# Shorter heads and ten Strassen pairs in a retention and HGRN2 layer on one core

## The chip, the core and the metric

The kernel runs on one core of a Trainium2 chip. The time is device microseconds of that core, from one launch of the whole layer. Five engines work side by side and meet through semaphores: TensorE (PE in the profile, its weight loads PEld), VectorE (DVE), ScalarE (ACT), GpSimd (POOL) and SyncE (SP), which here issues nearly all DMAs.

## The reference

One layer of a streaming encoder, in float32, for 1024 frames of a new stream and 8 x 16 frames of running streams (1152 frames in all, 9 tiles of 128), model width 1024:

```python
h = rms_norm(x, g_pre_mix)
z = h @ w_in                                   # 1024 x 10240
q_a, k_a, v_a, g_a, q_b, f_b, i_b, g_b, m_a, m_b = split(z)
# branch a: retention, 4 heads of 256, q and k rotated (rope), chunk-recurrent state
o_a = head_rms(retention(rope(q_a), rope(k_a) / 16, v_a, s_ret))
y_a = (silu(g_a) * o_a) @ w_a
# branch b: HGRN2, 8 heads of 128, forget gate f, state S_t = diag(f_t) S_(t-1) + k_t v_t^T
o_b = head_rms(hgrn2(q_b, 1 - f, i_b, log f, s_hgrn))
y_b = (silu(g_b) * o_b) @ w_b
x = x + rms_norm((sigmoid(m_a) * y_a + sigmoid(m_b) * y_b) @ w_out, g_post_mix)
u = square(relu(rms_norm(x, g_pre_ffn) @ w_up))
x = x + rms_norm(u @ w_down, g_post_ffn)
```

The outputs are x for both sets of frames and the new states of all heads.

## The kernel before

Every product in float32 is made of three products of the `fp32r` type: each operand is split into a high part (a rounded copy, made by ScalarE: `WHI`, `XH`) and a remainder (made by VectorE: `WLO`, `XL`), and the three cross products are summed in PSUM.

The input projection `z` is made in blocks of 128 output columns. Two kinds of block exist:
- a **plain block** (`gemm`) takes three **slots**, one for each chunk of 384 frames; a slot is 8 x 3 = 24 products of 384 columns. ScalarE copies each finished slot to `ZST` (`evac`), SyncE stores the block to `scratch_z`. For the next block ScalarE makes `WHI` and VectorE `WLO` (`wlo_block`), once in three slots.
- a **Strassen pair** (`strassen`) makes two blocks at once with seven half-size products instead of eight: 7 x 2 halves x 4 x 3 = 168 products of 288 columns. `NZ` pairs run in a stage of their own ahead of the retention; the pairs are the blocks of `z` that come first in `z_item`.

The heads of both branches have small products that depend on VectorE, ScalarE and GpSimd. They are woven into the plain blocks, so that TensorE has a slot of work between two dependent steps. The order is written out by hand as a function of the slot number `s` within a head:
- a retention head has `RET_BLOCKS` = 6 blocks, 18 slots. From slot `RA` = 7 on, tile `t` is started in slot 7 + t (`ret_a`: transpose of the keys, scores), finished in the next slot (`ret_b`: output and state, for the last tile `ret_b8` with the eight streams' states), and its output is transposed another slot later (`out_t`). Ahead of that VectorE rotates the head's queries (`rotate_q`, three chunks) and half of its keys (`rotate_k0`), GpSimd the other half. Then `q_ok` and `k_ok` let `ret_a` begin.
- an HGRN head has `HG_BLOCKS` = 4 blocks, 12 slots. Tiles are started in the slots `HG_A`, that is 0, 1, 2 and 4 to 9 (`hg_a`), with `hg_b` one slot and `out_t` two slots later. GpSimd prepares the decayed keys of each chunk of three tiles (`prep_k`), VectorE the queries (`prep_q`) and the score weights (`weights`), and the chunks 0 and 1 of the next head are begun in this head.
- behind the retention lie `GAP` = 2 blocks without head work.

Of each finished tile the path to its transpose is the same in both branches: ScalarE squares and sums (`head_sq`), VectorE makes the mean (`head_ms`, tile `OMS`), GpSimd takes the power -1/2 (`head_rs`, tile `ORS`), ScalarE scales the output (`head_scale`, tile `OT`), TensorE transposes it (`out_t`), VectorE multiplies with the gate (`gated`, tile `UB`).

Each engine works its instructions off in the order written. Behind the heads, from the block `NRB` on, follow the projections `w_a`, `w_b`, `w_out` and the feed-forward part, which the change leaves alone.

## Time and profile before

| | |
|---|---|
| runs timed | 2349.69, 2350.68, 2352.55 us; median 2350.68 |
| the profiled execution | 2349.41 us, its span 2347.6 us |
| mean granted clock of TensorE | 0.998 of full |
| busy share of the span | TensorE 99%, VectorE 59%, ScalarE 35%, GpSimd 20% |
| plain blocks of `z` and their products of 384 columns | 60, of them 58 behind the first stage; L942 to L944, 1776 of each |
| Strassen products of 288 columns | L1054 to L1057, 3360, for 6 pairs of `z` and 14 of the feed-forward part |

A busy time is the time in which at least one instruction of the engine ran; the durations of TensorE's products overlap (their ends are modelled), so what a product costs is read from start to start. A wait is put down to the instruction that came last.

### The profile page before, as it was taken

What the parts mean: (1) busy time and instruction counts of PE and PEld (TensorE: products, weight loads), DVE (VectorE), ACT (ScalarE), POOL (GpSimd) and SP (SyncE); (2) the same over time, 40 slices, a digit from 0 to 9 for tenths busy, and PEclk for the clock granted to TensorE, in tenths of its full rate; (3) what the DMA queues carried; (4) which work ended last, traced back from release to release, by engine and by line L of the source; (5) the groups of instructions that cost most, each with busy time, mean ns of one, the idle gap of its engine ahead of it and who ended that gap; (6) DMA issues with size and microseconds to landing.
All of it is one profiled execution on the core that took longest, in us unless ns stands there. A gap on an engine that the chain in (4) does not pass through costs nothing. (4 is left out here: it accounts for less than half of the span.)

```text
span 2347.6 us, 37061 instructions
## 1 busy us (share of the span) xinstructions
PE 2325.4 (99%) x14240; PEld 2184.5 (93%) x14240; DVE 1378.4 (59%) x2562; ACT 818.0 (35%) x1552; POOL 477.9 (20%) x732
## 2 busy tenths in 40 slices
PE   8999999999999999999999999999999999999998
PEld 7899999999999999999999999988999999888886
DVE  7434355362636777777776434556755556777575
ACT  5223232323222333333232332333555554333233
POOL 1000022221206666566655000000000000000002
PEclk9999999999999999999999999999999999999999
DMA  5212455353724343344334634222434436533424
GB/s 196 85 57 103 145 181 173 123 200 115 234 93 158 116 130 113 114 128 133 108 115 143 203 106 140 100 100 82 150 112 152 137 123 250 191 117 125 170 72 143
DMA packets 256044, 319.23 MB, mean 136 GB/s; under 512 B 10005, under 2 KB 200217, under 8 KB 255769
## 3 DMA queue, kind: packets, MB, share of 16 engines
q1 hardware_dynamic: 255464, 315.67, 40.1%
q0 software_dynamic: 432, 1.57, 0.4%
q8 instruction: 96, 1.57, 0.3%
q14 instruction: 52, 0.42, 0.1%
...
## 5 line engine op out<-in xcount | busy, mean ns | idle before, releaser
L942 PE MATMUL bank<-XH,WHI 128*128 128x384 f32 x1776 | 609.9, 343 | 1.6 <-issue 0.9
L944 PE MATMUL bank<-XH,WLO 128*128 128x384 f32 x1776 | 594.7, 335 | 0.0
L943 PE MATMUL bank<-XL,WHI 128*128 128x384 f32 x1776 | 593.9, 334 | 0.0
L942 PEld LDWEIGHTS bank<-XH,WHI 128*128 128x128 f32 x1776 | 333.8, 188 | 5.6 <-issue 2.4
L943 PEld LDWEIGHTS bank<-XL,WHI 128*128 128x128 f32 x1776 | 333.9, 188 | 0.8
L944 PEld LDWEIGHTS bank<-XH,WLO 128*128 128x128 f32 x1776 | 333.3, 188 | 0.0
L1396 ACT ACTIVATE ZST<-bank 128x384 f32<-128x384 f32 x180 | 88.3, 492 | 377.6 <-PE bank L944 371.8
L1330 PE MATMUL bank<-WSH,USH 128*128 128x512 f32 x448 | 175.3, 391 | 1.0 <-issue 1.0
L1332 PE MATMUL bank<-WSH,USL 128*128 128x512 f32 x448 | 175.3, 391 | 0.0
L1331 PE MATMUL bank<-WSL,USH 128*128 128x512 f32 x448 | 175.1, 391 | 0.0
L1396 ACT ACTIVATE WHI<-WRAW 128x1024 fp32r<-128x1024 f32 (+1 forms) x161 | 135.2, 842 | 114.0 <-PE bank L1057 70.3
L2604 POOL TENSOR_TENSOR ORS<-OMS,mhalf 128x1 f32<-128x1 f32 x108 | 69.8, 646 | 440.7 <-DVE OMS L2100 406.1
L2604 POOL TENSOR_TENSOR yrs<-yms,mhalf 128x1 f32<-128x1 f32 x9 | 9.4, 1215 | 708.0 <-DVE yms L2398 708.0
L1057 PE MATMUL bank<-XH,WLO 128*128 128x288 f32 x480 | 141.6, 295 | 0.0
L1057 PE MATMUL bank<-SXH,WXL 128*128 128x288 f32 x480 | 141.5, 295 | 0.0
L1056 PE MATMUL bank<-SXL,WXH 128*128 128x288 f32 x480 | 141.3, 294 | 0.0
L1056 PE MATMUL bank<-XL,WHI 128*128 128x288 f32 x480 | 141.3, 294 | 0.0
L1054 PE MATMUL bank<-SXH,WXH 128*128 128x288 f32 x480 | 141.3, 294 | 0.0
L1054 PE MATMUL bank<-XH,WHI 128*128 128x288 f32 x480 | 141.3, 294 | 0.0
L2055 DVE TENSOR_TENSOR U<-U,bank 128x288 f32<-128x288 f32 x120 | 54.3, 453 | 124.5 <-PE bank L1057 124.5
L1396 ACT ACTIVATE USH<-UOP 128x2048 fp32r<-128x2048 f32 x28 | 53.7, 1916 | 210.5 <-PE bank L1332 210.5
L1921 DVE TENSOR_TENSOR WLO<-WRAW,WHI 128x1024 fp32r<-128x1024 f32 x80 | 102.6, 1283 | 37.0 <-ACT WHI L1396 28.7
...
## 6 DMA issues: line engine op xcount, KB each, us to landing
...
```

Of the source, the lines that this page charges most:

```text
L942: pe.matmul(psum[c][:, 0:CH], WHI[p][:, k, :], XH[:, k, s], start=(k == 0), stop=False)
L943: pe.matmul(psum[c][:, 0:CH], WHI[p][:, k, :], XL[:, k, s], start=False, stop=False)
L944: last = pe.matmul(psum[c][:, 0:CH], WLO[p][:, k, :], XH[:, k, s], start=False, stop=(k == KT - 1))
L1054: pe.matmul(bank, wh[:, k, :], xh[:, k0 + k, ts], start=(fresh and k == 0), stop=False, skip_group_check=True)
L1056: pe.matmul(bank, wh[:, k, :], xl[:, k0 + k, ts], start=False, stop=False, skip_group_check=True)
L1057: last = pe.matmul(bank, wl[:, k, :], xh[:, k0 + k, ts], start=False, stop=(k == 3), skip_group_check=True)
L1330: pe.matmul(out, uh(k), wh[:, k, :], start=(fresh and k == 0), stop=False, skip_group_check=True)
L1331: pe.matmul(out, uh(k), wl[:, k, :], start=False, stop=False, skip_group_check=True)
L1332: last = pe.matmul(out, ul(k), wh[:, k, :], start=False, stop=(k == 3), skip_group_check=True)
L1396: return act.activation(dst, src, ACT.Copy)
L1921: dve.tensor_tensor(lo, src, plain(hi), ALU.subtract).then_inc(w_lo, 1)
L2604: return pool.tensor_tensor(dst, src, e, ALU.pow)
```

## The change

`NZ` goes from 6 to 10: four more Strassen pairs, eight plain blocks of `z` fewer. To have room for that, the heads get shorter: the retention has 21 blocks (6, 5, 5, 5 for its heads; `RA` becomes `RET_A`, 7 for head 0 and 4 for the others), the HGRN part 29 blocks with the two free ones ahead of it. HGRN heads no longer begin at a block's edge: seven have 10 slots, the last has 11, and `hg_slots` runs through them. Tile `t` is started in slot `t`, without a pause. The last tile's `out_t` falls into slot 0 of the next head.

What surrounds the heads moves with them. In the retention the stream states get a buffer of their own (`S8A` lay in `ZK`, the raw keys) and `KZ8` moves into `RTMP`, so that the next head's raw keys can be loaded from the fourth block of this head on. GpSimd rotates chunk 0 of the next head's keys ahead of the last tile's `head_rs` and chunks 1 and 2 behind it; VectorE rotates chunk 0 of the next head's queries in the last slot. In the HGRN part GpSimd takes the last tile's root of the old head within `prep_k` of chunk 1, and tile 0's root behind that `prep_k`. The loops over heads and pairs of heads that were rolled on the engines (`Fori`) are now written out.

```diff
@@ -38,14 +38,16 @@
 PAST = 512
 EPS = 1e-6
 
-RET_BLOCKS = 6
-RET_SLOTS = RET_BLOCKS * NC
-HG_BLOCKS = 4
-HG_SLOTS = HG_BLOCKS * NC
-RA = 7
-HG_A = (0, 1, 2, 4, 5, 6, 7, 8, 9)
-R_GATE = (7, 8, 13)
-H_GATE = (0, 2, 6)
+RET_LEN = (6, 5, 5, 5)
+RET_AT = (0, 6, 11, 16)
+RET_BLOCKS = sum(RET_LEN)
+HG_BLOCKS = 29
+HG_START = 6
+HG_LEN = (10, 10, 10, 10, 10, 10, 10, 11)
+HG_AT = [None] * HG_START + [(h, s) for h, n in enumerate(HG_LEN) for s in range(n)]
+RET_A = tuple(NC * n - 11 for n in RET_LEN)
+R_GATE = (0, 1, 6)
+H_GATE = (1, 2, 6)
 BW = P + TS
...
@@ -57,8 +59,7 @@
 NGD = 4
 NPL = 2
 NQ = FF // 256
-GAP = 2
-NZ = 7 - GAP // 2
+NZ = (72 - 2 - RET_BLOCKS - HG_BLOCKS) // 2
 NP = NZ + NQ - NPL
 VT = 2 * NT
...
@@ -180,8 +181,8 @@
         ZETA, G128, G16 = (HC[:, 4 * P + i:4 * P + i + 1] for i in range(3))
         SR = sb("SR", [P, 2, RD], F32, pr)
         S8B = sb("S8B", [P, 4, 2, RD], F32, pr)
-        S8A = ZK[:, :, :].rearrange("p a t -> p (a t)")[:, 0:4 * 2 * RD].rearrange("p (b d e) -> p b d e", b=4, d=2)
-        KZ8 = [sb(f"KZ8{i}", [P, RD], F32, pr) for i in range(2)]
+        S8A = sb("S8A", [P, 4, 2, RD], F32, pr)
+        KZ8 = [RTMP[:, :, :].rearrange("p a n -> p (a n)")[:, b * RD:(b + 1) * RD] for b in range(2)]
         pr.close()
...
@@ -328,8 +329,21 @@
 
         zs, us, x1s = scr["z"], scr["u"], scr["x1"]
         uqs, u8s, vs = scr["uq"], scr["u8"], scr["v"]
-        NRB = 2 + RET_BLOCKS * RH + GAP + HG_BLOCKS * HH
-        NHB = NRB - HG_BLOCKS * HH
+        NHB = 2 + RET_BLOCKS
+        NRB = NHB + HG_BLOCKS
+
+        def hg_slots():
+
+            for q, at in enumerate(HG_AT):
+                yield NHB + q // NC, q % NC, *(at or (None, None))
+
+        def hg_out(h, s):
+
+            if h is None:
+                return None
+            if s == 0:
+                return (h - 1, NT - 1) if h and HG_LEN[h - 1] == NT + 1 else None
+            return (h, s - 2) if 2 <= s < NT + 2 else None
         NB1 = NRB + 2 * KT
         W_OUT = NB1
         W_FFN = W_OUT + KT
...
@@ -652,26 +666,30 @@
                 sp.dma_start(HC[:, 0:2 * P], a["c_ret"][h, :, 0:2 * P]).then_inc(R.in_[0], 16)
                 sp.dma_start(ZQ[:, :, :], ret_z(h, 0)).then_inc(R.in_[0], 16)
 
+            def load_rk(h):
+
+                sp.dma_start(ZK[:, :, :], ret_z(h, 1)).then_inc(R.in_[1], 16)
+
             for i in range(2):
                 sp.wait_ge(z_st[i], 16)
             load_rq(0)
             for h in range(RH):
-                for j in range(RET_BLOCKS):
-                    n = 2 + RET_BLOCKS * h + j
...
@@ -703,11 +719,15 @@
                         for d in range(2):
                             sp.dma_start(S8B[:, :, d, :], a["state_ret"][0, 4:8, h, d * P:(d + 1) * P, :]
                                          .rearrange("b p e -> p b e")).then_inc(R.s8_in[1], 16)
+                    if j == late + 3 and h < RH - 1:
+                        sp.wait_ge(R.k_ok, h + 1)
+                        sp.wait_ge(R.q_ok, h + 1)
+                        z_stored(6 * h + 9 - 2 * NZ)
+                        load_rk(h + 1)
                     for c in range(2):
-                        if j == (4, 5)[c]:
+                        if j == late + (3, 4)[c]:
                             ret_store(h, c)
                 if h < RH - 1:
-                    z_stored(RET_BLOCKS * h + 7 - 2 * NZ)
                     sp.wait_ge(R.o_full, 9 * h + 8)
                     load_rq(h + 1)
                 else:
...
@@ -1149,10 +1174,12 @@
                     last = pe.transpose(PRB[:, e * P:(e + 1) * P], OT[:, e * P:(e + 1) * P], ident[:, :])
                 last.then_inc(K.ot, 1)
 
-            with pe.Fori(0, RH) as h:
-                for s in range(RET_SLOTS):
+            for h in range(RH):
+                RA = RET_A[h]
+                for s in range(NC * RET_LEN[h]):
                     j, c = divmod(s, NC)
-                    gemm(2 + RET_BLOCKS * h + j, None, j % 2, c)
+                    n = 2 + RET_AT[h] + j
+                    gemm(n, None, n % 2, c)
...
-                    if s in HG_A:
-                        hg_a(h, HG_A.index(s))
-                    if s - 2 in HG_A:
-                        out_t(H, h, HG_A.index(s - 2), 1)
-                    if s - 1 in HG_A:
-                        hg_b(h, HG_A.index(s - 1))
+            for n, c, h, s in hg_slots():
+                gemm(n, None, n % 2, c)
+                if (h, s) == (0, 0):
+                    pe.wait_ge(R.kv, 8 * RH + 1)
+                    pe.wait_ge(R.kz8, 2 * RH + 1)
+                    pe.wait_ge(R.att, 9 * RH + 1)
+                    pe.wait_ge(R.o_ev, 9 * RH + 1)
+                    pe.wait_ge(R.st_ev, 16 * RH + 1)
+                    pe.wait_ge(R.um, 9 * RH + 1)
+                if h is None:
+                    continue
+                if s < NT:
+                    hg_a(h, s)
+                if hg_out(h, s):
+                    out_t(H, *hg_out(h, s), 1)
+                if 1 <= s < NT + 1:
+                    hg_b(h, s - 1)
...
@@ -2139,16 +2155,18 @@
 
             dve.wait_ge(c_in, 48)
             dve.wait_ge(qxb0, 1)
-            with dve.Fori(0, RH) as h:
-                for s in range(RET_SLOTS):
+            for h in range(RH):
+                RA = RET_A[h]
+                for s in range(NC * RET_LEN[h]):
                     j, c = divmod(s, NC)
-                    n = 2 + RET_BLOCKS * h + j
+                    n = 2 + RET_AT[h] + j
                     if c == 0:
-                        wlo_block(n + 1, (j + 1) % 2)
+                        wlo_block(n + 1, (n + 1) % 2)
                     if s < 3:
-                        if s == 0:
-                            dve.wait_ge(R.in_[0], 32 * h + 32)
-                        rotate_q(h, s)
+                        if s == 0 and h == 0:
+                            dve.wait_ge(R.in_[0], 32)
+                        if s or h == 0:
+                            rotate_q(h, s)
                     if s == 3:
                         dve.wait_ge(R.in_[1], 16 * h + 16)
                         for c in range(NC):
@@ -2161,6 +2179,9 @@
                             dve.wait_ge(R.sc, 9 * h + t + 1)
                             dve.wait_ge(R.st_full, 16 * h + (t if t >= 2 else 1))
                             dve.tensor_tensor(ATT[t % 2][:, :], PSC[:, 0:P], DM[:, t // NTP, :], ALU.mult).then_inc(R.att, 1)
+                    if s == NC * RET_LEN[h] - 1 and h < RH - 1:
+                        dve.wait_ge(R.in_[0], 32 * h + 64)
+                        rotate_q(h + 1, 0)
                     if RA + 2 <= s < RA + 2 + NT:
                         gated(R, h, s - RA - 2, 2)
                     for t in range(NT):
...
@@ -2622,24 +2631,35 @@
             ch(pool.memset(QXB[:, :, :], 0.0))
             ch.reset()
             pool.sem_inc(qxb0, 1)
-            with pool.Fori(0, RH) as h:
-                pool.wait_ge(R.in_[1], 16 * h + 16)
-                pool.wait_ge(R.att, 9 * h + 1)
-                for c in range(NC):
-                    s = slice(c * CH, (c + 1) * CH)
-                    cs, sn = CS[:, 0, s], CS[:, 1, s]
-                    pool.tensor_tensor(PTMP[:, 0, :], ZK[:, 0, s], sn, ALU.mult)
-                    ch(pool.tensor_tensor(PTMP[:, 1, :], ZK[:, 1, s], cs, ALU.mult))
-                    last = pool.tensor_tensor(KR[:, 1, s], PTMP[:, 0, :], PTMP[:, 1, :], ALU.add)
-                    if c < NC - 1:
-                        ch(last)
-                last.then_inc(R.k_ok, 1)
+            def rotate_k1(c):
+
+                s = slice(c * CH, (c + 1) * CH)
+                cs, sn = CS[:, 0, s], CS[:, 1, s]
+                pool.tensor_tensor(PTMP[:, 0, :], ZK[:, 0, s], sn, ALU.mult)
+                ch(pool.tensor_tensor(PTMP[:, 1, :], ZK[:, 1, s], cs, ALU.mult))
+                last = pool.tensor_tensor(KR[:, 1, s], PTMP[:, 0, :], PTMP[:, 1, :], ALU.add)
+                if c < NC - 1:
+                    ch(last)
+                else:
+                    last.then_inc(R.k_ok, 1)
+
+            pool.wait_ge(R.in_[1], 16)
+            for c in range(NC):
+                rotate_k1(c)
+            for h in range(RH):
                 for c in range(2):
                     gate(R, h, c, 2, ZG[c][:, :, :])
                 for t in range(NT):
+                    if t == NT - 1 and h < RH - 1:
+                        pool.wait_ge(R.in_[1], 16 * h + 32)
+                        pool.wait_ge(R.att, 9 * h + 10)
+                        rotate_k1(0)
                     head_rs(R, h, t)
                     if t == 4:
                         gate(R, h, 2, 2, ZG[0][:, :, :])
+                if h < RH - 1:
+                    for c in range(1, NC):
+                        rotate_k1(c)
                 ch.reset()
 
             ret_mixed(pool)
...
@@ -2687,39 +2707,33 @@
                 ch(pool.tensor_tensor(KRH[:, s], KK[:, s], RR[:, s], ALU.mult))
...
-                        pool.wait_ge(H.att, 9 * h + 10)
-                        head_rs(H, h, 8)
-                    ch.reset()
+            def rs(h, t):
+                return lambda: head_rs(H, h, t)
+
+            def hgate(h, c):
+                gate(H, h, c, 1, HZ[3][:, c * CH:(c + 1) * CH].unsqueeze(1))
 
             prep_k(0, 0, 0)
             ch.reset()
-            with pool.Fori(0, HH // 2 - 1) as i:
-                hg_pair(i, False)
-            hg_pair(HH // 2 - 1, True)
+            for h in range(HH):
+                first = {0: rs(h - 1, NT - 1)} if h else {}
+                prep_k(h, 1, (h + 1) % 2, {**first, 5: lambda: hgate(h, 0)})
+                head_rs(H, h, 0)
+                hgate(h, 1)
+                head_rs(H, h, 1)
+                head_rs(H, h, 2)
+                pool.wait_ge(H.att, 9 * h + 4)
+                prep_k(h, 2, h % 2, {4: rs(h, 3)})
+                head_rs(H, h, 4)
+                hgate(h, 2)
+                if h < HH - 1:
+                    pool.wait_ge(H.att, 9 * h + 7)
+                    prep_k(h + 1, 0, (h + 1) % 2, {0: rs(h, 5), 3: rs(h, 6), 6: rs(h, 7)})
```

VectorE, the seam between two retention heads, before: the end of the loop over heads and, behind the branch, its start (`OMS` is the last tile's mean, `UB` its gated product, `RTMP`, `QR` the rotation of queries).

```order
L2183 SCALAR_TENSOR_TENSOR S8B<-S8B,HC,bank 128x512
L2100 TENSOR_SCALAR OMS<-OSS 128x1
L2110 TENSOR_TENSOR UB<-bank,SG 128x2x128
...
L1921 TENSOR_TENSOR WLO<-WRAW,WHI 128x1024
L2150 ISA
L2117 TENSOR_TENSOR RTMP<-ZQ,CS 128x384
L2118 TENSOR_TENSOR RTMP<-ZQ,CS 128x384
```

The same place now, from head 0 to head 1.

```order
L2204 SCALAR_TENSOR_TENSOR S8B<-S8B,HC,bank 128x512 x2
L2116 TENSOR_SCALAR OMS<-OSS 128x1
L2133 TENSOR_TENSOR RTMP<-ZQ,CS 128x384
...
L2142 TENSOR_TENSOR ZQ<-QR,HC 128x384 x2
L2126 TENSOR_TENSOR UB<-bank,SG 128x2x128
L85 ISA
L1937 TENSOR_TENSOR WLO<-WRAW,WHI 128x1024
L2133 TENSOR_TENSOR RTMP<-ZQ,CS 128x384
```

One of the three rotations of queries moved ahead of the gated product; the other two and all rotations of keys still stand behind the weight remainder `WLO`.

GpSimd at that place, now (`PTMP`, `KR` the rotation of keys, three rows a chunk; `ORS` the roots). Before, all nine rows of the rotation stood together at the head's start, ahead of its gates `SG`, and behind the last root stood nothing.

```order
L2613 TENSOR_TENSOR ORS<-OMS,mhalf 128x1 x3
L2638 TENSOR_TENSOR PTMP<-ZK,CS 128x384
L2639 TENSOR_TENSOR PTMP<-ZK,CS 128x384
L2640 TENSOR_TENSOR KR<-PTMP 128x384
L2613 TENSOR_TENSOR ORS<-OMS,mhalf 128x1
L2638 TENSOR_TENSOR PTMP<-ZK,CS 128x384
```

Three rows moved ahead of the last tile's root, six stand right behind it.

GpSimd in the HGRN part, before: the end of `prep_k` of chunk 1 (`RR` the running products, `KRH` its last result).

```order
L2673 TENSOR_TENSOR KE<-KK,RR 128x3x64
L2682 TENSOR_TENSOR RR<-RR,FT 128x3x64
L2618 ISA
L2604 TENSOR_TENSOR ORS<-OMS,mhalf 128x1
L2687 TENSOR_TENSOR KRH<-KK,RR 128x384
L2614 TENSOR_TENSOR SG<-SG,HZ 128x384
```

The same `prep_k` now, its start and its end, from head 0 to head 1.

```order
L2678 TENSOR_TENSOR FT<-HZ 128x192
L2679 MEMSET RR 128x384
L2702 TENSOR_TENSOR RR<-RR,HZ 128x192
L2613 TENSOR_TENSOR ORS<-OMS,mhalf 128x1
L2687 TENSOR_TENSOR KE<-KK,RR 128x384
...
L2693 TENSOR_TENSOR KE<-KK,RR 128x3x64
L2702 TENSOR_TENSOR RR<-RR,FT 128x3x64
L2707 TENSOR_TENSOR KRH<-KK,RR 128x384
L2613 TENSOR_TENSOR ORS<-OMS,mhalf 128x1
```

The root of tile 0 stood ahead of `KRH` and now stands behind it; the root near the start is that of the old head's last tile.

## Rows read from the trace of the kernel before

The rows are whole lines of the profile. A timeline row is: start and duration in us, engine, line of the kernel, operation, output and inputs by name, shapes, how many, and in brackets the engine's idle time ahead of it and what ended it.

**Rows 1.** The page of the kernel before: its span and the busy time of TensorE

```profile
span 2347.6 us, 37061 instructions
PE 2325.4 (99%) x14240; PEld 2184.5 (93%) x14240; DVE 1378.4 (59%) x2562; ACT 818.0 (35%) x1552; POOL 477.9 (20%) x732
```

**Rows 2.** TensorE's waits over the whole span: total, times, longest, us

```profile
PE bank L1149 <- ACT OT L1602: 1.2, 1, 1.2
PE bank L942 <- issue: 0.9, 1, 0.9
PE bank L942 <- DVE WLO L1921: 0.8, 1, 0.8
```

**Rows 3.** TensorE in order of time (start, duration, us): plain products, then Strassen products

```profile
36.21 0.33 PE L963 MATMUL bank<-XL,WHI 128*128 128x384 f32 x1
...
46.09 0.33 PE L963 MATMUL bank<-XL,WHI 128*128 128x384 f32 x1
...
148.11 0.29 PE L1056 MATMUL bank<-XL,WHI 128*128 128x288 f32 x1
...
151.69 0.29 PE L1056 MATMUL bank<-XL,WHI 128*128 128x288 f32 x1
```

**Rows 4.** VectorE in order of time, from retention head 0 to head 1

```profile
387.18 0.14 DVE L2100 TENSOR_SCALAR OMS<-OSS 128x1 f32<-128x1 f32 x1
389.56 0.42 DVE L2110 TENSOR_TENSOR UB<-bank,SG 128x256 f32<-128x256 f32 x1 [2.23 <-PE bank L1149]
392.26 1.23 DVE L1921 TENSOR_TENSOR WLO<-WRAW,WHI 128x1024 fp32r<-128x1024 f32 x1 [2.28 <-ACT WHI L1396]
393.41 0.55 DVE L2117 TENSOR_TENSOR RTMP<-ZQ,CS 128x384 f32<-128x384 f32 x1
...
398.83 0.56 DVE L2119 TENSOR_TENSOR QR<-RTMP 128x384 f32<-128x384 f32 x1
...
403.20 1.25 DVE L2119 TENSOR_TENSOR QR<-RTMP 128x384 f32<-128x384 f32 x1
...
418.96 0.56 DVE L2138 TENSOR_TENSOR KR<-RTMP 128x384 f32<-128x384 f32 x1
```

**Rows 5.** TensorE at the same seam: first gemm, first transpose of keys

```profile
389.27 0.42 PE L942 MATMUL bank<-XH,WHI 128*128 128x384 f32 x1
...
422.67 0.38 PE L1078 MATMUL bank<-ident,KR 128*128 128x128 f32 x2
```

**Rows 6.** GpSimd at the same seam: first and last of nine products for the keys

```profile
402.96 1.08 POOL L2631 TENSOR_TENSOR PTMP<-ZK,CS 128x384 f32<-128x384 f32 x1 [15.01 <-DMA ZK<-scratch_z]
...
412.84 1.89 POOL L2633 TENSOR_TENSOR KR<-PTMP 128x384 f32<-128x384 f32 x1
```

**Rows 7.** TensorE, from one HGRN head to the next

```profile
941.31 0.44 PE L942 MATMUL bank<-XH,WHI 128*128 128x384 f32 x1
...
963.38 0.27 PE L1149 MATMUL bank<-ident,OT 128*128 128x128 f32 x1
```

**Rows 8.** GpSimd, key preparation of chunk 1 at the same seam

```profile
943.75 0.74 POOL L2604 TENSOR_TENSOR ORS<-OMS,mhalf 128x1 f32<-128x1 f32 x1 [4.72 <-remote]
944.59 0.51 POOL L2658 TENSOR_TENSOR FT<-HZ 128x192 f32<-128x192 f32 x1
...
948.54 0.60 POOL L2675 TENSOR_TENSOR KE<-KK,RR 128x192 f32<-128x192 f32 x1
...
950.18 1.45 POOL L2675 TENSOR_TENSOR KE<-KK,RR 128x192 f32<-128x192 f32 x1
...
959.85 0.59 POOL L2604 TENSOR_TENSOR ORS<-OMS,mhalf 128x1 f32<-128x1 f32 x1 [2.47 <-DVE OMS L2100]
960.42 1.16 POOL L2687 TENSOR_TENSOR KRH<-KK,RR 128x384 f32<-128x384 f32 x1
```

**Rows 9.** VectorE's weight remainder in that stretch; ScalarE's scaling of one tile

```profile
949.91 1.27 DVE L1921 TENSOR_TENSOR WLO<-WRAW,WHI 128x1024 fp32r<-128x1024 f32 x1 [0.21 <-DVE PP L2202]
...
817.62 0.37 ACT L1602 ACTIVATE OT<-bank,ORS 128x128 f32<-128x128 f32 x1 [2.49 <-POOL ORS L2604]
```

363 lines of the change are left out of this document (159 added, 204 removed).

## The prediction

> **What bounds the kernel now.** I read the head of the page first: the span, and which engine fills it [rows 1]. TensorE is busy for 2325.4 us of 2347.6, and it runs at the full clock (2.4 GHz) all through. The list of TensorE's waits comes next: of its ten rows only three lie between the first plain block and the end of the last HGRN head, 0.9 and 0.8 us where the plain blocks begin and 1.2 us behind the last head [rows 2]. No retention head and no other HGRN head makes TensorE wait. So each microsecond of products that goes away is gained, as long as VectorE and GpSimd, which now finish ahead of TensorE, still do so in shorter heads. The other views are the timelines of the two seams where a head follows a head [rows 4 to 9], for there the room is smallest.
>
> **The products.** Eight plain blocks go and four Strassen pairs come. In the timeline of TensorE a plain product of 384 columns starts every 0.173 us (19 groups of three between the two rows, 9.88 us, 0.520 each), a Strassen product of 288 columns every 0.1326 us (nine groups, 3.58 us, 0.398 each) [rows 3]. Two plain blocks are 144 products or 48 groups, 24.96 us; one pair is 168 products or 56 groups, 22.28 us. The gain is 2.68 us a pair, four times 2.68 = **10.7 us**. The bounds of this term are narrow (10 to 11): both kinds of product already run without gaps.
>
> The Trainium skill (TensorE: Matmul & The Clock Gate, section Back-to-back issue gap) gives N/2.4 + 2.5 ns for a warm product and warns that a stream with weight loads is spaced by both. By the formula alone a plain pair would be 23.4 us, a Strassen pair 20.6, and the gain 11.3 us instead of 10.7. The rows stand 10 ns above the formula at both widths, and the sum goes by the rows.
>
> A gemm slot (one chunk of a block, 24 products) is eight groups, 4.16 us. A retention head goes from 18 slots to 15, an HGRN head from 12 to 10; the head's own small products stay. Head 0 of the retention keeps its 18 slots, and so do the two blocks ahead of HGRN.
>
> **First seam: one retention head to the next (three times).** The last stream product is behind us, and VectorE's last mean square of the head ends at 387.3 [rows 4]. TensorE starts the next head's first gemm at 389.27 and has eight gemms before it asks for the rotated queries and keys (389.27 + 33.3 = 422.6; it does so at 422.67) [rows 5]. VectorE is ready at 419.5, so there is room. In the changed kernel there are only five gemms: 389.27 + 5 x 4.16 = **410.1**. What has VectorE to do until then? One rotation of queries now stands in the last slot, ahead of the gated product, but the sum is what counts, since every piece stands in one queue:
> - three rotations of queries, one weight remainder, three rotations of keys: from 393.41 to 419.5 [rows 4], 26.1 us
> - the remainder ahead of them, 392.26 to 393.41: 1.15
> - the gated product that now stands between: 0.35 (its row says 0.42, overlapped at its end)
> That is 27.6 us. But GpSimd's nine products for the other half of the keys ran in it [rows 6], and they hurt: the same VectorE operation is 0.56 us without them and 1.25 with them [rows 4], so about 0.73 each, 6.6 in all. Three of the nine now run ahead of the seam, six are left to run right behind the reciprocal root of the last tile, so into this stretch. 27.6 - 3 x 0.73 = 25.4 us, and 387.3 + 25.4 = **412.7**. TensorE waits 2.6 us, with 0.1 for the signal **2.7 us**, and three seams make **8.1 us**. It falls to nothing if the six products cost VectorE nothing (387.3 + 21.1 = 408.4, ahead of 410.1), and grows to 4.9 a seam (14.7) if the contention of all nine is still paid. I take the middle because the six are sure to fall there.
>
> The Trainium skill (GPSIMD Engine Reference, section Specifications) says the same of the cause: GpSimd's way to SBUF is shared with VectorE, and they collide when VectorE reads two SBUF inputs. The trace agrees: the rotations, with two such inputs, go from 0.56 to 1.25 us. It speaks against this change, which leaves more of the two engines' work side by side.
>
> What the change moves in DMA hides: the keys for the next head are loaded five slots ahead, and the queue's stores wait some 2 us longer at the seam (the gated product is later). The values' load then still has over ten us before 410.1.
>
> **Second seam: one HGRN head to the next (seven times).** The long piece is GpSimd's key preparation of chunk 1 of the next head, which starts when the head's last state is out. It starts at 944.59 and ends at 961.58 (960.42 + 1.16), and holds a wait of 2.47 us for tile 0's mean square and that tile's reciprocal root, 0.59 [rows 8]. The change takes tile 0's root out of it (it now stands behind it) and puts the old head's last root in (0.74 [rows 8]). Without waits: 16.99 - 2.47 - 0.59 + 0.74 = 14.7 us, so it ends at 959.3; then tile 0's root, 959.9, ScalarE's scaling of the tile, 0.37 with 0.03 ahead of it [rows 9], **960.3**. TensorE wants that tile for its transpose. Before, it did so at 963.38, with four gemms behind 941.31 [rows 7]; now with three: 963.38 - 4.16 = **959.2**. It waits **1.1 us**. One thing varies: a weight remainder on VectorE stretches one GpSimd operation from 0.6 to 1.45 us [rows 8, 9]. With ten slots a head and three a block it falls into the stretch in heads 2, 3, 5 and 6, and behind its end in heads 1, 4 and 7; there 1.1 - 0.85, about 0.3 us, is left. Four times 1.1 and three times 0.3 are 5.3 us. Head 0 has the free blocks ahead and waits for nothing. Further down the head each tile now follows in the very next slot (the pause at slot 3 is gone), with little room for the queries of chunk 2 and for the roots of tiles 5 and 7; I put 0.2 us on each of eight heads for it, 1.6 us, a choice between 0 and 0.4. Together **6.9 us**, from 0 (the chain 1.1 us shorter) to some 14 (one more stretched operation a head: 7 x 0.85 more).
>
> **Costed at nothing.** The rolled loops become straight code: TensorE's waits for issue are 0.9 us at one place, elsewhere the queues run ahead. The stream states' own buffer: their load waits for their own store only. Four more pairs in the first Strassen stage: that stage has no wait inside now, its helpers have the same share per pair. The tail of the last head keeps its three last slots as they were.
>
> **Sum.** -10.7 + 8.1 + 6.9 = **+4.3 us** on the profiled execution's own 2349.4 us (span 2347.6 and 1.8 around it), 2353.7. The median of the runs shown, 2350.7, is 1.3 above that execution, so I predict **2355.0 us**, +0.18%. A measurement of this kernel tells about 0.2% (4.7 us) from no change.
>
> **Rivals.**
> 1. The gain arrives whole: both seams have the room, 2350.7 - 10.7 = 2340.0. For it speaks that TensorE waits nowhere in a head today; against it the two sums, which both come out late by one to three microseconds. Chance 0.12.
> 2. Only one seam is late. Only VectorE's: 2348.1. Only GpSimd's: 2346.9. For it: each sum is late by a margin of one or two stretched operations (0.73 or 0.85 us). Chance 0.23.
> 3. Slower beyond doubt: contention between VectorE and GpSimd at both seams. If all nine operations' worth is paid (14.7) and each of the seven HGRN seams has one more stretched operation (5.3 + 6.0 + 1.6 = 12.9), the sum is +16.9, 2367.6. It decides from 0.1 us more a stretched operation on: then already +4.7 is passed. For it: heads with less idle time put more of the two engines' work side by side. Against: the rows already hold the contention of nearly the same neighbours. Chance 0.15.
>
> **How the numbers follow.** The forecast, both seams late by about the sums (2349 to 2361), has 0.50. The range that holds 8 in 10 leaves out rival 1 and the far end of rival 3: **2345 to 2365**. Slower by over 0.2% (above 2355.4) is the upper half of the forecast, half of 0.50 less a little, 0.24, with rival 3, 0.15, and some of what I don't see (a missed wait can only add), 0.04: 0.43. Faster by over 0.2% (below 2346.0) is rival 1 and the lower part of rival 2: 0.19. Within 0.2%: 0.38.
>
> **What would show it.** In the profile after: 20 pairs become 24 in the two Strassen stages, the first stage some 89 us longer; TensorE waits in the retention for VectorE's rotated keys three times, 2 to 3 us each, at the fifth gemm of heads 1 to 3; in the HGRN heads for ScalarE's scaled tile, released by GpSimd's root, at slot 2, about 1 us in four heads and less in three. Right behind the mean square of the last retention tile GpSimd's products are 1.2 us long and VectorE's rotations too. The prediction is wrong if these waits are missing (the work had more room than the rows of its neighbours say), if a seam is late for a DMA instead (values or keys not landed), or if a wait stands where I costed nothing, such as the queries of chunk 2 in slot 6.

## The result and the profile after

| | kernel before | changed kernel |
|---|---|---|
| median | 2350.38 us (4 runs, 2349.69 to 2352.55) | 2371.20 us (4 runs, 2369.70 to 2372.92) |
| span of the profiled execution | 2347.6 us | 2370.1 us |
| ratio | | 1.0087 (95% interval 1.0073 to 1.0101) |

The changed kernel is 20.8 us slower. The forecast was 2355.0 with a range from 2345 to 2365, so it lies outside the range, on the side that the forecast had called the likeliest.

The busy time of each engine from the head of the page, as for the kernel before [rows 1]:

```profile
PE 2329.7 (98%) x14336; PEld 2181.5 (92%) x14336; DVE 1401.4 (59%) x2622; ACT 813.5 (34%) x1573; POOL 466.0 (20%) x732
```

TensorE has less to compute and is busy for longer, 2329.7 us instead of 2325.4. Then TensorE's waits (us in total, times, longest), which had only three rows in this part of the program before [rows 2]:

```profile
PE bank L1103 <- issue: 10.6, 3, 3.8
...
PE bank L1174 <- ACT OT L1626: 3.9, 9, 1.2
...
PE bank L1249 <- DVE UB L2126: 2.3, 3, 0.8
PE bank L967 <- DVE WLO L1937: 2.3, 1, 2.3
...
PE bank L1207 <- DVE ATT L2249: 0.9, 2, 0.5
```

L1103 is the first transpose of a retention head's keys, L1174 the transpose of a scaled tile, L1249 the stream-state products at the end of an HGRN head, L1207 the first transpose of an HGRN tile. These are 18 us of new waits. Against the gain of the products (12.6 us, read below) that makes some 5 us, not 21, so the list does not explain the loss. Four readings explain most of it.

**The products** gave what they should. TensorE in order of time, the first product of the first Strassen stage and the first plain product behind it, changed kernel:

```profile
150.17 0.29 PE L1079 MATMUL bank<-XH,WHI 128*128 128x288 f32 x1
...
373.42 0.41 PE L967 MATMUL bank<-XH,WHI 128*128 128x384 f32 x1 [0.55 <-issue]
```

and in the kernel before:

```profile
147.98 0.29 PE L1054 MATMUL bank<-XH,WHI 128*128 128x288 f32 x1
...
282.52 0.44 PE L942 MATMUL bank<-XH,WHI 128*128 128x384 f32 x1 [0.85 <-issue]
```

The stage is 223.25 us for ten pairs instead of 134.54 for six: 88.71 for four, 22.18 a pair. (The waits at the end of the two stretches, 0.55 and 0.85 us, are in these numbers; without them a pair is 22.25.) For them 24 slots went, 9 in the retention at 4.16 us and 15 in the HGRN heads. There a slot costs a little more, because small products stand on both sides of it. This slot of the kernel before, ahead of tile 0's transpose, lasts 949.89 - 945.63 = 4.26 us:

```profile
945.63 0.42 PE L942 MATMUL bank<-XH,WHI 128*128 128x384 f32 x1
...
949.89 0.27 PE L1180 MATMUL bank<-ident,HZ 128*128 128x128 f32 x1
```

The mean of all 84 slots of the seven periods is 4.26 us too. So 37.4 + 63.9 - 88.7 = 12.6 us were gained, and 20.8 + 12.6 = 33.4 us lost elsewhere.

**The retention seams.** TensorE at the end of the fifth gemm of head 1, ahead of the keys:

```profile
502.50 0.34 PE L969 MATMUL bank<-XH,WLO 128*128 128x384 f32 x1
506.68 0.66 PE L1103 MATMUL bank<-ident,KR 128*128 128x128 f32 x2 [3.84 <-issue]
```

The row names no signal ("issue"). TensorE asks for several here, and VectorE in the same stretch shows which of them came last (first row: the last mean square of head 0):

```profile
479.68 0.15 DVE L2116 TENSOR_SCALAR OMS<-OSS 128x1 f32<-128x1 f32 x1
...
482.13 1.25 DVE L2136 TENSOR_TENSOR RTMP<-ZQ,CS 128x384 f32<-128x384 f32 x1
...
491.71 0.56 DVE L2136 TENSOR_TENSOR RTMP<-ZQ,CS 128x384 f32<-128x384 f32 x1
...
501.74 2.07 DVE L2152 TENSOR_TENSOR RTMP<-ZK,CS 128x384 f32<-128x384 f32 x1
...
505.96 0.56 DVE L2154 TENSOR_TENSOR KR<-RTMP 128x384 f32<-128x384 f32 x1
```

The last key is done at 506.52, and TensorE starts at 506.68. The same operation of VectorE takes 1.25 us while GpSimd still rotates and 0.56 later, as the prediction had it. From the mean square (479.83) that is 26.7 us, where the prediction had 25.4. What it had not counted is GpSimd's gated product, which falls beside the rotation of 2.07 us:

```profile
501.39 2.00 POOL L2623 TENSOR_TENSOR SG<-SG,ZG 128x768 f32<-128x768 f32 x1 [13.25 <-ACT SG L1631]
```

**The clock behind the seams.** Windows of the changed kernel (length, busy us of each engine, the granted clock as PEclk, DMA share, GB/s), right behind the first, the second and the third wait:

```profile
506.60:509.00 2.40, 2.32 (x10) 2.35 (x11) 0.29 (x1) 1.21 (x2) 0.34 (x1) 0.50 0.92 235
509.00:512.00 3.00, 3.00 (x11) 3.00 (x10) 0.00 (x0) 0.00 (x0) 1.50 (x1) 0.50 0.00 0
...
606.60:610.00 3.40, 3.40 (x22) 3.40 (x23) 0.29 (x1) 1.21 (x2) 1.69 (x1) 1.00 0.43 106
703.60:706.50 2.90, 2.90 (x13) 2.90 (x14) 0.29 (x1) 1.21 (x2) 1.26 (x1) 0.55 0.57 144
```

Behind the first wait TensorE runs at 0.50, which is 1.2 GHz, and is busy all the time: 11 products in 3.00 us where the second seam shows 22 in 3.40. Behind the third it is halved for most of the window. TensorE had stood still for 3.84, 3.45 and 3.32 us before. The Trainium skill (TensorE: Matmul & The Clock Gate, section What's actually happening) names these two levels, 1.2 and 2.4 GHz, and the rows agree. In the list of waits this loss is not seen, because TensorE is busy in it. It is one part of why TensorE's busy time grew; the other is the hidden waits of the next reading, for E2 below has a busy time of 2330.0 us without a halved stretch in its heads. From the first transposes of the four heads (409.36, 506.68, 606.57, 703.51) the three head periods are 294.15 us, and 3 x 105.70 - 37.4 = 279.7 were due: 14.5 us lost, and about 1.7 more behind the third wait, 16.2 us in all, of which 10.6 are the waits.

**The HGRN heads.** The stream-state products come once a head. First rows of head 0 and head 7, changed kernel and kernel before:

```profile
865.92 0.50 PE L1249 MATMUL bank<-KVT,SG 32*128 32x128 f32 x8 [0.75 <-DVE UB L2126]
...
1321.24 0.39 PE L1249 MATMUL bank<-KVT,SG 32*128 32x128 f32 x4
```

```profile
797.80 0.39 PE L1222 MATMUL bank<-KVT,SG 32*128 32x128 f32 x4
...
1297.83 0.39 PE L1222 MATMUL bank<-KVT,SG 32*128 32x128 f32 x4
```

Seven periods are 455.3 us; 500.0 less 14 slots of 4.26 would be 440.4. **14.9 us** are lost, while the list of waits has only some 6 us of new ones in these heads. The rest is in waits that end while the product before them still counts as busy: a small product is busy for 0.33 us by its record and the next one starts 0.11 behind it, so a delay of up to about 0.2 us gives no idle time and a longer one is shown too short. Start against start shows them. This is TensorE at tile 0 of head 2:

```profile
947.80 0.27 PE L1207 MATMUL bank<-ident,HZ 128*128 128x128 f32 x1
...
950.33 0.33 PE L1174 MATMUL bank<-ident,OT 128*128 128x128 f32 x1 [0.80 <-ACT OT L1626]
...
951.20 0.42 PE L967 MATMUL bank<-XH,WHI 128*128 128x384 f32 x1
...
955.47 0.27 PE L1207 MATMUL bank<-ident,HZ 128*128 128x128 f32 x1
...
957.73 0.42 PE L967 MATMUL bank<-XH,WHI 128*128 128x384 f32 x1
```

The small products of this slot last 951.20 - 947.80 = 3.40 us, the same ones of the next slot 957.73 - 955.47 = 2.26, so the delay is 1.1 us and not 0.80. Head 5 has the same; in heads 1, 4 and 7 the slot of tile 0 lasts 2.47 to 2.49 us, 0.2 too long, and in heads 3 and 6 2.29 and 2.31. GpSimd, first product of the key preparation and tile 0's root:

```profile
934.56 0.51 POOL L2678 TENSOR_TENSOR FT<-HZ 128x192 f32<-128x192 f32 x1 [4.66 <-DVEq L2262]
...
949.32 0.55 POOL L2613 TENSOR_TENSOR ORS<-OMS,mhalf 128x1 f32<-128x1 f32 x1 [0.18 <-POOL KRH L2707]
```

GpSimd stands idle for 4.66 us because VectorE makes the forget gates of chunk 1 only behind the eight stream-state updates (2.16 us) and the mean square:

```profile
931.42 2.16 DVE L2291 SCALAR_TENSOR_TENSOR SH<-SH,PP,bank 128x128 f32<-128x128 f32 x8 [1.38 <-PE bank L1249]
...
933.55 0.47 DVE L2259 TENSOR_SCALAR HZ<-HZ,LBC 128x384 f32<-128x384 f32 x1
```

The rest items are 1.5 us from the first plain block to the first transpose of keys (VectorE's weight remainder, 2.3 us of wait instead of 0.8), 1.2 us between the last retention seam and the stream-state products of HGRN head 0, beyond the clock's 1.7 (0.75 of them is the wait in the row at 865.92, the rest I did not follow), and 0.9 us gained behind those of head 7, which I did not follow either. Sum: -12.6 + 16.2 + 14.9 + 1.5 + 1.2 - 0.9 = +20.3, where the medians say 20.8. The spans of the two profiled executions differ by 22.5; the 2.2 us between lie ahead of the first Strassen stage, which starts at 147.98 and 150.17, and anywhere from 147.2 to 150.2 in the traces of the experiments.

### The profile page after: what moved, and what is told of

Read it like the earlier page. It is cut to its first block, busy times and chain, and to the rows that moved or that the text cites. A ratio compares the mean times of both kernels' runs of the same rounds, so it can differ in the third digit from the quotient of the medians.

```text
span 2370.1 us, 36477 instructions
## 1 busy us (share of the span) xinstructions
PE 2329.7 (98%) x14336; PEld 2181.5 (92%) x14336; DVE 1401.4 (59%) x2622; ACT 813.5 (34%) x1573; POOL 466.0 (20%) x732
## 4 chain that ended last, share of the span: by engine, by line
PE 88%; DVE 5%; POOL 3%; issue 3%; DMA 1%; ACT 0%; SPq 0%; DVEq 0%; POOLq 0%
PE bank L967 10%; PE bank L969 9%; PE bank L968 9%; PE bank L1082 7%; PE bank L1081 7%; PE bank L1079 7%; PE bank L1354 5%; PE bank L1356 5%; PE bank L1355 5%; PE bank L1043 1%; PE bank L1325 1%; PE bank L1041 1%; PE bank L1323 1%; PE bank L1324 1%; PE bank L1042 1%
## 5 line engine op out<-in xcount | busy, mean ns | idle before, releaser
L967 PE MATMUL bank<-XH,WHI 128*128 128x384 f32 x1584 | 545.9, 345 | 2.8 <-DVE WLO L1937 2.3
L969 PE MATMUL bank<-XH,WLO 128*128 128x384 f32 x1584 | 531.8, 336 | 0.0
L968 PE MATMUL bank<-XL,WHI 128*128 128x384 f32 x1584 | 531.1, 335 | 0.0
L967 PEld LDWEIGHTS bank<-XH,WHI 128*128 128x128 f32 x1584 | 299.4, 189 | 6.5 <-DVE WLO L1937 2.6
L968 PEld LDWEIGHTS bank<-XL,WHI 128*128 128x128 f32 x1584 | 298.9, 189 | 0.8
L969 PEld LDWEIGHTS bank<-XH,WLO 128*128 128x128 f32 x1584 | 298.4, 188 | 0.0
L1420 ACT ACTIVATE WHI<-WRAW 128x512 fp32r<-128x512 f32 (+1 forms) x169 | 136.8, 811 | 133.5 <-PE bank L1082 90.0
L1082 PE MATMUL bank<-XH,WLO 128*128 128x288 f32 x576 | 169.9, 295 | 0.0
L1626 ACT ACTIVATE OT<-bank,ORS 128x128 f32<-128x128 f32 (+1 forms) x108 | 43.6, 404 | 292.2 <-POOL ORS L2613 292.2
L2040 DVE TENSOR_TENSOR WLO<-WRAW,WHI 128x512 fp32r<-128x512 f32 x96 | 66.0, 689 | 115.4 <-ACT WHI L1420 115.3
```

Of the source, the lines that this page charges most:

```text
L967: pe.matmul(psum[c][:, 0:CH], WHI[p][:, k, :], XH[:, k, s], start=(k == 0), stop=False)
L968: pe.matmul(psum[c][:, 0:CH], WHI[p][:, k, :], XL[:, k, s], start=False, stop=False)
L969: last = pe.matmul(psum[c][:, 0:CH], WLO[p][:, k, :], XH[:, k, s], start=False, stop=(k == KT - 1))
L1082: last = pe.matmul(bank, wl[:, k, :], xh[:, k0 + k, ts], start=False, stop=(k == 3), skip_group_check=True)
L1420: return act.activation(dst, src, ACT.Copy)
L2040: dve.tensor_tensor(WOP[i][1], op_raw(s, i), plain(WOP[i][0]), ALU.subtract).then_inc(uo_lo, 1)
```

## Experiments

All times are medians beside runs of the kernel before on the same chip; ratios are to these. Where two changed kernels are compared, their medians can come from different rounds; the kernel before lay between 2350.38 and 2351.02 us in them, so such a difference is uncertain by some 0.6 us.

**E1, retention heads short alone.**

```diff
-HG_BLOCKS = 29, HG_START = 6, HG_LEN = (10, 10, 10, 10, 10, 10, 10, 11)
+HG_BLOCKS = 35, HG_START = 9, HG_LEN = (12, 12, 12, 12, 12, 12, 12, 12)
```

> Retention heads as in the changed kernel (18, 15, 15, 15 slots), HGRN heads of 12 slots, three free blocks ahead of them, 7 pairs in the first Strassen stage. Against the kernel before: six plain slots fewer (six times 4.16 us) and one pair more (22.2), so -2.8 us of products. Theory (the retention seams cost what the trace of the changed kernel shows: three waits of 3.3 to 3.8 us, and about 4 us in two stretches at 1.2 GHz behind them): +14.5, so about 2362 us, ratio 1.005, with the same three waits and two halved stretches. Rival (the halved clock belongs to that one execution): +10.6 only, 2358. Rival (the loss sits in the HGRN heads): below 2352.

Measured: 2385.16 us, ratio 1.0145 (1.0128 to 1.0162). The retention part came as expected: waits of 11.4 us in three, and the periods lose 15.7 us. But the total is 23 us above the expectation, and neither rival says so either. The loss sits in the HGRN heads, where nothing was shortened against the kernel before: six of the seven periods are 74.3 to 74.4 us instead of 71.4. TensorE and GpSimd at slot 10 of one of them:

```profile
969.47 0.33 PE L1174 MATMUL bank<-ident,OT 128*128 128x128 f32 x1 [1.60 <-ACT OT L1626]
```

```profile
966.77 0.51 POOL L2678 TENSOR_TENSOR FT<-HZ 128x192 f32<-128x192 f32 x1 [6.13 <-DVEq L2262]
...
968.46 0.55 POOL L2613 TENSOR_TENSOR ORS<-OMS,mhalf 128x1 f32<-128x1 f32 x1
```

The last tile's root stands inside the key preparation, behind its first products, and these wait 6.13 us for the forget gates. In heads of 10 slots this hides, but not because the last tile goes out a slot later (as E11's expectation has it): both transposes come one gemm behind the stream-state products. In the changed kernel the next head's tile 0 stands between, and its small products fill the time:

```profile
935.49 0.27 PE L1207 MATMUL bank<-ident,HZ 128*128 128x128 f32 x1
...
937.27 0.33 PE L1174 MATMUL bank<-ident,OT 128*128 128x128 f32 x1
```

From the stream-state products to this transpose it is 6.7 us in both kernels (930.56 to 937.27 there, 962.77 to 969.47 in E1). So the experiment was not clean, and it shows that the new order is itself a cost.

**E2, HGRN heads short alone.**

```diff
-RET_LEN = (6, 5, 5, 5)
-RET_AT = (0, 6, 11, 16)
+RET_LEN = (6, 6, 6, 6)
+RET_AT = (0, 6, 12, 18)
...
-HG_BLOCKS = 29
-HG_START = 6
+HG_BLOCKS = 30
+HG_START = 9
```

> HGRN heads as in the changed kernel (10 slots, the last 11), retention heads of 18 slots in the new order of work, three free blocks, 8 pairs in the first Strassen stage. Against the kernel before: 12 slots fewer (15 of 4.26 us go, 3 free ones of 4.16 come, -51.4) and two pairs more (+44.4), -7.0 us of products. Theory (each HGRN head of ten slots costs 1.7 to 3.0 us of lateness, as its periods in the changed kernel's trace say, 15 us in all, more than the list of TensorE's waits shows): 2358 us, ratio 1.0035, and no wait and no halved clock in the retention. Rival (only the listed waits of 5 us count): 2348.

Measured: 2358.58 us, ratio 1.0032 (1.0019 to 1.0044): the theory's 2358, not the rival's 2348. No wait for keys is left in the list and the mean granted clock is 0.999. The seven HGRN periods are 454.9 us. So the HGRN heads lose some 15 us by themselves, more than twice what the list shows.

**E3, keys early in the retention.**

VectorE rotates chunks 0 and 1 of the next head's keys ahead of tile 8's mask, GpSimd chunk 0 ahead of the root of tile 7 and chunk 1 ahead of that of tile 8. ScalarE writes `KZ8` only behind tile 8's mask, since it lies in `RTMP`.

```diff
+                act.wait_ge(R.att, 9 * h + NT + 1)
...
-                        for c in range(NC):
+                        for c in range(2 if h else 0, NC):
                             rotate_k0(c)
...
+                    if s == RA + NT - 1 and h < RH - 1:
+                        dve.wait_ge(R.in_[1], 16 * h + 32)
+                        for c in range(2):
+                            rotate_k0(c)
...
+                    if t == NT - 2 and h < RH - 1:
+                        pool.wait_ge(R.in_[1], 16 * h + 32)
+                        pool.wait_ge(R.att, 9 * h + 8)
+                        rotate_k1(0)
                     if t == NT - 1 and h < RH - 1:
-                        pool.wait_ge(R.in_[1], 16 * h + 32)
+                        rotate_k1(1)
                         pool.wait_ge(R.att, 9 * h + 10)
-                        rotate_k1(0)
...
-                    for c in range(1, NC):
-                        rotate_k1(c)
+                    rotate_k1(2)
```

> The changed kernel, but two of the three rotations of the next head's keys on VectorE stand ahead of tile 8's mask, where it has 4 us of idle time, and two of GpSimd's three stand behind the reciprocal roots of tiles 6 and 7. About 3.3 us of VectorE's 26.7 us in the seam go, and three GpSimd products instead of six run beside it (2.2 us less). Theory (VectorE's queue in the seam is what TensorE waits for, and the halved clock follows from these waits): the three waits fall below 0.5 us each, no stretch at 1.2 GHz, about 15 us less than the changed kernel, 2356. Rival (the halved clock has another cause, such as the DMA at the seam): waits gone, clock still halved, 2361. Rival (a DMA or the stream states is next in line): waits of over 2 us stay, 2366 or more.

Measured: 2355.06 us, ratio 1.0019 (1.0009 to 1.0029), 16.1 less than the changed kernel. TensorE in order of time at the same seam:

```profile
503.60 0.38 PE L1103 MATMUL bank<-ident,KR 128*128 128x128 f32 x2
```

and VectorE's last key product:

```profile
499.63 0.56 DVE L2155 TENSOR_TENSOR KR<-RTMP 128x384 f32<-128x384 f32 x1
```

Its last key is ready at 500.2, 3.4 us ahead of TensorE. The windows behind the seam have the full clock, though the DMA share is as high as before (1.03 and 1.10), which takes the rival of the DMA away:

```profile
500.00:503.60 3.60, 3.60 (x23) 3.57 (x21) 0.19 (x1) 0.87 (x2) 1.84 (x1) 1.00 1.03 376
503.60:507.00 3.40, 3.40 (x23) 3.40 (x22) 0.29 (x1) 1.59 (x3) 1.53 (x1) 1.00 1.10 320
```

But this trace has a halved stretch at another place. In the first plain block TensorE waits for the weight remainder, and behind that the clock is at 0.50:

```profile
400.13 0.69 PE L967 MATMUL bank<-XH,WHI 128*128 128x384 f32 x1 [2.12 <-DVE WLO L1938]
```

```profile
399.00:400.11 1.11, 0.00 (x0) 0.00 (x0) 1.11 (x2) 0.48 (x1) 0.00 (x0) 1.00 0.00 0
400.11:403.52 3.41, 3.39 (x11) 3.40 (x12) 3.27 (x7) 0.00 (x0) 0.00 (x0) 0.50 0.53 152
```

So a wait of 2.12 us can be followed by 1.2 GHz too, and with the DMA at rest ahead of its end. E1, E7, E10 and E11 show the same behind this wait (2.1 to 2.3 us); the changed kernel and six others, with waits of the same length there, do not.

**E4, forget gates ahead of the stream states.**

```diff
+if s == 9 and h < HH - 1: forget(h + 1, 1)
 if 1 <= s < NT + 1: hg_state(h, s - 1); head_ms(...)
...
-if s == 9: forget(h + 1, 1)
```

> The changed kernel, but in slot 9 of an HGRN head VectorE makes the next head's forget gates of chunk 1 ahead of the eight stream-state updates, not behind them. GpSimd's key preparation waits for them (4.7 us idle behind the head's last state) and could start about 2.5 us earlier. Theory (the lateness of slots 0 to 3 comes down this chain): the waits at tile 0 in heads 2 and 5 (0.8 us each in the list, 1.1 in the starts) and the one at the mask of tile 0 in heads 3 and 6 shrink, 3 to 5 us less than the changed kernel, 2367. Rival (VectorE and GpSimd only collide elsewhere): within 1 us of the changed kernel, 2371.

Measured: 2367.94 us, ratio 1.0074 (1.0057 to 1.0091), 3.3 less than the changed kernel. In its trace tile 0's waits in heads 2 and 5 are gone (waits for OT 2.0 us instead of 3.9), but the mask waits in heads 3 and 6 stayed (1.2 instead of 0.9): the theory's size, with half of its detail wrong. The seven HGRN periods fell by 4.9 us, from 455.3 to 450.5. The total fell by less. One reason is in this execution's retention: its three periods are 1.7 us longer than the changed kernel's, and the clock is halved behind all three seams and not behind two.

**E5, both repairs.**

> The changed kernel with the repairs of both seams together: keys rotated ahead of tile 8's mask (alone 16.1 us) and the forget gates ahead of the stream states (alone 3.3 us). Theory (two separate causes at two separate places): the gains add, 2371.2 - 19.4 = 2352. Rival (they share a cause, VectorE's collisions with GpSimd): 2355, no better than the first alone.

Measured: 2350.86 us, ratio 1.0004 (0.9994 to 1.0014). They add (16.1 + 3.3 = 19.4, measured 20.3): two causes at two places. Beside E3 the forget gates are worth 4.2 us.

**E6, weight remainder late.** E5, and VectorE's `wlo_block` at the head of a block's first slot moved behind that slot's `head_ms`.

> The previous kernel, but in HGRN slots that begin a block VectorE makes the weight remainder (1.25 us, wanted three slots later) behind the slot's gated product, state and mean square, not ahead of its masks. Theory (heads 0, 3 and 6 wait at slot 9 for the gated product of tile 7, and heads 3 and 6 at slot 1 for tile 0's mask, because the remainder stands ahead of them): these five waits go, 3 x 0.8 + 2 x 0.75 = about 4 us, 2348. Rival (the remainder then delays the query work behind it by as much): 2352.

Measured: 2358.15 us, ratio 1.0034 (1.002 to 1.0049), 7.3 us more than E5. Both theory and rival missed. VectorE and TensorE at slot 6 of head 1:

```profile
892.40 1.22 DVE L1938 TENSOR_TENSOR WLO<-WRAW,WHI 128x1024 fp32r<-128x1024 f32 x1
...
894.79 0.42 DVE L2235 TENSOR_TENSOR QP<-HZ,PP 128x256 f32<-128x256 f32 x1
```

```profile
895.48 0.30 PE L1207 MATMUL bank<-ident,HZ 128*128 128x128 f32 x1 [0.97 <-DMA HZ<-scratch_z]
```

The remainder used to run in VectorE's idle time while TensorE was in its gemm (in E5 at 883.52, and behind it VectorE still waited 0.98 us for TensorE); now it stands ahead of the queries of chunk 2, which end at 895.21, and TensorE waits for them (the row names a DMA, but that chunk was loaded by transfers issued from 845.84 on, 50 us before). Other slots have the same with masks and roots; I did not follow each.

**E7, roots early.** E5, and on GpSimd:

```diff
-prep_k(h, 2, h % 2, {4: rs(h, 3)})
+prep_k(h, 2, h % 2, {3: rs(h, 3)})
...
-prep_k(h + 1, 0, (h + 1) % 2, {0: rs(h, 5), 3: rs(h, 6), 6: rs(h, 7)})
+head_rs(H, h, 5)
+prep_k(h + 1, 0, (h + 1) % 2, {2: rs(h, 6), 5: rs(h, 7)})
```

> The keys-and-forget kernel, but GpSimd takes its reciprocal roots where the mean squares are ready: tile 5 ahead of the next head's key preparation of chunk 0 (it stands idle there for 5 us and takes the root 2.9 us after the mean square), tiles 6, 7 and 3 one level earlier. Theory (half of the HGRN lateness is many small waits of 0.25 to 0.55 us for the scaled tile, mostly too short for the list of waits, 2.5 us in three heads): about 6 us less, 2346. Rival (delays that the list does not show are no delays, the spacing of small products merely varies): 2351 or more.

Measured: 2347.49 us, ratio 0.9986 (0.9976 to 0.9996), 3.4 less than E5, and every one of its runs is below every one of E5's; the seven HGRN periods go from 450.7 to 447.7, while the listed waits of these heads fall by only some 0.6 us. So delays that the list does not show are delays, but they were half of what I had summed.

**E8, all four edits.**

> All four repairs. If they are separate, 2352 - 4 - 6 = 2342, 8 to 9 us less than the kernel before, ratio 0.9965; the ten pairs then give nearly all their products' gain (13 us by the trace of the changed kernel: 24 slots of 4.2 us against 88.7 us). If they share their effect, 2345 to 2347.

Measured: 2353.58 us, ratio 1.0013 (1.0003 to 1.0023). The edit of E6 costs 6.1 us here too; the expectation rested on its gain.

**E9 and E10, the two halves of E3.** E9 moves only GpSimd's products, E10 only VectorE's.

> The changed kernel with only GpSimd's part of the early keys: its three products for chunk 1 stand behind the root of tile 7, not in the seam; VectorE's order is as in the changed kernel. A dose between the changed kernel and the one with all early keys. In that one VectorE's chain from the last mean square to the last key was 19.7 us instead of 26.8: 3.3 us for the two rotations moved, about 2.1 for three products' contention, 1.5 because GpSimd's gated product then falls behind the chain. Theory (six products beside VectorE cost it 0.7 us each): the three waits shrink by about 2.1 us, to 1.2 to 1.7 each, and if a stretch at 1.2 GHz needs a wait of three microseconds, none is left: 2371.2 - 6.3 - 5.1 = 2360. Rival (shorter waits still halve the clock): 2365. Rival (contention costs VectorE nothing): 2371.

> The changed kernel with only VectorE's part of the early keys. VectorE's queue in the seam is 3.3 us shorter, the contention stays. Theory: waits of 0.3 to 0.6 us, no stretch at 1.2 GHz, 2371.2 - 9 to 10 - 5 = 2356 to 2357. Rival (another wait stands right behind it): above 2360.

Measured: E9 2360.50 us, ratio 1.0039 (1.0025 to 1.0054); E10 2355.48 us, ratio 1.0019 (1.001 to 1.0029). E9 came as the theory had it, in time and waits. E10 has no wait for keys left, where the theory had 0.3 to 0.6 us each, and is half a microsecond below its 2356. It is as fast as E3, so with VectorE's part done GpSimd's part adds nothing. E9's first line of waits, and its windows behind the three seams:

```profile
PE bank L1103 <- issue: 5.0, 3, 1.7
```

```profile
502.00:505.50 3.50, 3.34 (x22) 3.37 (x23) 0.29 (x1) 1.21 (x2) 1.61 (x1) 1.00 0.68 174
597.20:600.50 3.30, 3.11 (x20) 3.14 (x21) 0.32 (x2) 1.21 (x2) 1.37 (x1) 1.00 0.78 212
692.40:696.00 3.60, 3.48 (x22) 3.52 (x23) 0.29 (x1) 1.21 (x2) 1.75 (x1) 1.00 0.62 163
```

Three GpSimd products less a seam, and nothing changed on VectorE's list, shorten TensorE's wait by 5.6 / 3 = 1.9 us, 0.62 for each product (GpSimd's gated product still falls beside the rotation of keys there, as in the changed kernel: the longest product is 2.09 us in E9's first seam and 2.18 in its second). The Trainium skill (GPSIMD Engine Reference, section Specifications) says that GpSimd shares its way to SBUF with VectorE; this run agrees and gives the price. The clock stays at 1.00 in all three windows, so of the 10.7 us by which E9 is below the changed kernel 5.6 are waits, and the 5.1 left are put down to the clock. The changed kernel's trace has 10.2 us at half the clock at its seams, all but 0.8 of them with TensorE at work, which is 4.7 us and agrees.

**E11, E1 with the forget gates first.**

> The kernel with short retention heads and HGRN heads of 12 slots (2385.2, far above the 2362 expected), with the forget gates ahead of the stream states. Its trace shows TensorE waiting 1.8 us in each HGRN head, at slot 10, for the last tile: GpSimd's root of tile 8 stands behind the first products of the key preparation, which wait for forget gates that VectorE makes behind the stream states. Theory (the new order of roots was laid out for heads of 10 slots, where the last tile goes out a slot later): these eight waits go, about 14 us less, 2371; seven waits of 0.8 us for tile 7's gated product stay. Rival (the free slots or the longer heads cost by themselves): 2380 or more.

Measured: 2373.27 us, ratio 1.0096 (1.0079 to 1.0112), 11.9 less than E1. Of the waits for OT in these heads 0.2 us are left; the seven of up to 0.8 us for tile 7's gated product stayed (5.1 us). The seven periods are 507.3 us, 519.4 in E1 and 500.0 before, so 5.1 of the 7.2 us that are left are in these waits, and E1 is explained but for 2 us. The windows behind its three keys' waits (up to 4.0 us) show the halved clock again:

```profile
438.80:442.00 3.20, 3.02 (x12) 3.05 (x13) 0.31 (x2) 1.21 (x2) 1.04 (x1) 0.54 0.67 171
537.60:541.00 3.40, 3.27 (x13) 3.30 (x14) 0.29 (x1) 1.21 (x2) 1.29 (x1) 0.54 0.61 155
636.70:640.50 3.80, 3.68 (x16) 3.71 (x17) 0.29 (x1) 1.21 (x2) 1.70 (x1) 0.60 0.56 148
```

**E12, queries a slot later.** E7, and VectorE's three `prep_q` pieces of chunk 1 in slots 0, 1 and 2:

```diff
-if s < 2: prep_q(1, (h + 1) % 2, s + 1)
+if s < (3 if h else 2): prep_q(1, (h + 1) % 2, s if h else s + 1)
...
-if s == 9: prep_q(1, h % 2, 0)
```

> The kernel with early keys, forget gates and roots (2347.5), and the three query pieces of chunk 1 stand in slots 0, 1 and 2 of the head, not in slot 9 of the head before and slots 0 and 1. VectorE is then ahead at slots 0 and 1, where heads 3 and 6 wait 0.75 us for tile 0's mask and heads 2 and 5 0.3 to 0.6, but the last piece must be ready for slot 3 and is close in heads where a weight remainder falls into slot 2 (1, 4 and 7). Theory (five to six waits at masks are due to these pieces): 2 to 3 us less, 2345. Rival (the wait moves to slot 3, as the remainder moved to the queries of chunk 2): 2348 to 2352.

Measured: 2346.11 us, ratio 0.9978 (0.9969 to 0.9988), 1.4 less than E7, and the waits for masks fell from 1.3 to 0.3 us. E7's and E12's intervals overlap, so between these two I go by the trace: seven periods are 446.6 us instead of 447.7.

E12 is the fastest kernel here, 4.9 us below the kernel before. Of the products' 12.6 us some 6 are still lost in the HGRN periods (446.6 against 440.4), 1.5 at the first plain block and about 1 ahead of HGRN head 0; the 0.9 behind the last head is gained.

## Why the prediction was wrong

- **Sign and direction** were right: products gained, both seams late, more lost than gained. The size was wrong by 16.5 us (20.8 instead of 4.3).
- **The products, -10.7: too small.** Measured -12.6. The pair was right (22.28 said, 22.25 without the waits). The term took a slot at eight groups of 0.52 us everywhere; in the HGRN heads it is 4.26, which is 1.5 us for 15 slots, and 0.3 is the shorter wait behind the stage. The bounds "10 to 11" left out the change between kinds of product.
- **First seam, +8.1: mechanism right, mis-sized, and one consequence missing.** VectorE's queue was the cause (E10), contention at about 0.62 us for each GpSimd product part of it (E9; the sum had 0.73, its own rows 1.25 - 0.56 = 0.69), and no DMA. The waits were 10.6 us instead of 8.1, because GpSimd's own product for the gates (its L2623), which the sum did not list, costs a rotation 1.5 us. What the prediction nowhere priced is that TensorE ran at half its clock behind two of the three waits: 5.1 us more by E9, 5.5 by E3. Measured in all 16.1 (E3).
- **Second seam, +6.9: the priced event came true in part, the unpriced ones cost more.** The chain was sized well: GpSimd's preparation took 14.6 us (14.7 said), and tile 0 was 1.1 us late in heads 2 and 5 and 0.2 us in heads 1, 4 and 7 (0.3 said). In heads 3 and 6, where 1.1 was said, it was not late; there TensorE waited for tile 0's mask. The step that failed is "further down the head ... I put 0.2 us on each of eight heads for it, 1.6 us". Measured are 14.9 us in seven periods, of which tile 0's transpose is about 3 (5.3 said). What can be given a cause is what an edit took away: 4.1 to 4.9 us with the forget gates moved ahead, tile 0's waits among them (E4, E5), 2.9 us roots placed behind products that themselves wait for VectorE (E7), 1.1 us masks behind query pieces (E12). The 6.2 us that are left no run takes away; the list of E12 shows 2.8 of them, as waits for scaled tiles (1.4), gated products (1.1) and masks (0.3), and the rest stays open. I had looked at margins for one tile and taken the other slots as they were, though the pause at slot 3 was gone and each had less room. And the queries of chunk 2, which I feared, make no wait in the changed kernel's list; they were late as soon as the remainder stood ahead of them (E6).
- **GpSimd's start** was taken as "when the head's last state is out". It is VectorE's forget gates that release it, and where these stand in VectorE's order is worth 3.3 us (E4), 4.2 beside the early keys (E5 against E3).
- **Costed at nothing:** of this the written-out loops hold (TensorE's wait for issue at the first plain block is 0.5 us instead of 0.9), the stream states' buffer shows in no wait, and the time behind the last head is 0.9 us shorter. The first plain block does not hold: 1.5 us more for the weight remainder.
- **Rival 3** (contention at both seams, 2367.6, chance 0.15) was the nearest in time. Its mechanism is only a part of the cause, and the range stopped short of it.
